# Hybrid decoder step on one core: the second dense group of a tick is placed straight behind the first

## What is computed

```python
def decoder_layer(x, c, attend, conv_prev, ...):
    sh1, sc1, gt1, sh2, sc2, gt2 = ada_mod(c, w_ada, b_ada)
    h = rms_norm(x, rms_g1) * (1 + sc1) + sh1
    q, k, v, hc, bgate, cgate, ga, gb = project_in(h, w_in, q_norm_g, k_norm_g)
    o_att = attend(q, k, v, sb_bias)
    yc, conv_state = short_conv(cgate * hc, conv_prev, conv_w, conv_b)
    x = x + gt1 * merge_branches(o_att, bgate * yc, ga, gb, w_att_out, w_conv_out, w_o)
    h2 = rms_norm(x, rms_g2) * (1 + sc2) + sh2
    x = x + gt2 * sqrelu_mlp(h2, w_mlp1, w_mlp2)
    return x, k, v, conv_state

def stick_breaking(z, valid):          # z = q.k/8 + bias
    log_beta = jax.nn.log_sigmoid(z)
    log_keep = jnp.where(valid, jax.nn.log_sigmoid(-z), 0.0)
    suffix = lax.cumsum(log_keep, axis=z.ndim - 1, reverse=True) - log_keep
    return jnp.where(valid, jnp.exp(log_beta + suffix), 0.0)
```

## Time and profile before

| | us |
|---|---|
| median of 3 runs | 1870.39 (1869.11 to 1870.75) |
| the profiled execution | 1871.02 |
| its span, first to last instruction | 1869.2 |
| TensorE busy | 1777.9 (95%) |
| VectorE busy | 878.6 (47%) |
| GpSimd busy | 659.8 (35%) |
| ScalarE busy | 299.3 (16%) |
| mean granted TensorE clock | 0.966 |

### The profile page before, as it was taken

One profiled execution on the slowest core, in us unless ns is written; L12 is line 12 of the kernel. 1 busy time (PEld: TensorE's weight loads), 2 busy tenths in 40 slices (PEclk: granted clock), 3 DMA queues, 4 the chain that ended last, 5 costly groups with the idle time before them and its releaser, 6 DMA issues. The chain is left out here.

```text
span 1869.2 us, 29718 instructions
## 1 busy us (share of the span) xinstructions
PE 1777.9 (95%) x11934; PEld 1657.0 (89%) x11934; DVE 878.6 (47%) x1425; ACT 299.3 (16%) x583; POOL 659.8 (35%) x377
## 2 busy tenths in 40 slices
PE   7999998997989999999898969999999999999999
PEld 6989777776778887879898868999999999999999
DVE  1434155545444444432783246555454545455553
ACT  3123211010101111111210123201020202020200
POOL 1037034343424443442342213433333333333332
PEclk8699999998989999999999989999999999999999
DMA  6312064444544665643432101111111111111112
GB/s 218 118 55 79 35 223 165 155 161 137 196 144 156 227 205 183 212 150 127 186 138 93 45 23 35 46 46 46 46 48 53 47 46 46 46 46 46 46 46 93
DMA packets 72505, 196.83 MB, mean 105 GB/s; under 512 B 8081, under 2 KB 8210, under 8 KB 72370
## 3 DMA queue, kind: packets, MB, share of 16 engines
q1 hardware_dynamic: 67682, 179.76, 28.6%
q10 hardware_dynamic: 4688, 15.18, 2.1%
HBM read 175.41 MB, written 19.50 MB: 104 GB/s over the span
## 5 line engine op out<-in xcount | busy, mean ns | idle before, releaser
L523 POOL TENSOR_TENSOR wh<-raw,zero 128x1024 fp32r<-128x1024 f32 x116 | 220.0, 1897 | 789.0 <-PE bank L589 700.3
L525 POOL TENSOR_TENSOR wl<-raw,wh 128x1024 fp32r<-128x1024 f32 x116 | 285.2, 2458 | 9.1
L589 PE MATMUL bank<-hH,wh 128*128 128x352 f32 x816 | 280.5, 344 | 3.0 <-POOL wl L525 3.0
L589 PE MATMUL bank<-hL,wh 128*128 128x352 f32 x816 | 266.5, 327 | 0.0
L589 PE MATMUL bank<-hH,wl 128*128 128x352 f32 x816 | 266.0, 326 | 0.0
L589 PE MATMUL bank<-h2H,wh 128*128 128x352 f32 x768 | 248.4, 323 | 0.9 <-issue 0.9
L1303 DVE SCALAR_TENSOR_TENSOR act<-bank,mods,act 128x352 f32<-128x352 f32 (+1 forms) x216 | 122.3, 571 | 268.0 <-PE bank L589 262.0
L589 PE MATMUL bank<-hidH,wh 128*128 128x352 f32 x768 | 247.7, 323 | 0.0
L589 PE MATMUL bank<-h2H,wl 128*128 128x352 f32 x768 | 246.3, 321 | 0.0
L550 POOL TENSOR_TENSOR beta<-beta,kb 128x512 f32<-128x512 f32 (+3 forms) x96 | 122.5, 1296 | 350.9 <-DVE kb L1132 350.9
L589 PE MATMUL bank<-hidH,wl 128*128 128x352 f32 x768 | 246.3, 321 | 0.0
(11 more groups left out here) (147 smaller groups left out, 2667.9 us busy)
## 6 DMA issues: line engine op xcount, KB each, us to landing
raw<-in_weights SPq DMA_DIRECT2D x168, 512.0 KB, 3.6
ring<-in_cache_k SPq DMA_DIRECT2D x128, 256.0 KB, 4.0
ring<-in_cache_v SPq DMA_DIRECT2D x128, 256.0 KB, 3.6
gate_scratch<-gt ACTq DMA_DIRECT2D x16, 528.0 KB, 3.7
act<-gate_scratch SPq DMA_DIRECT2D x16, 528.0 KB, 4.5
xt<-in_xT SPq DMA_DIRECT2D x8, 528.0 KB, 9.0
act<-in_xT SPq DMA_DIRECT2D x8, 528.0 KB, 4.5
out_yT<-act SPq DMA_DIRECT2D x8, 528.0 KB, 2.7
```

The costliest lines, as they stand in the source:

```text
L523: mark(pool.tensor_tensor(wh[u % 2][:, :], src[:, :], zero[:, 0:1].to_broadcast([P, 1024]), ALU.add))
L525: pool.tensor_tensor(wl[u % 2][:, :], src[:, :], wh[u % 2][:, :].bitcast(F32), ALU.subtract)\
L589: mm = pe.matmul(out, x, y, start=n == 0, stop=n == end)
```

## The change

In a tick with two dense groups, the second now comes directly behind the first on TensorE, ScalarE, VectorE and GpSimd, ahead of `sample_turn`, `sample_scores` and `turn`. `SLOTS`, from which the order of loads is made, is changed alike. No instruction is added or removed.

```diff
-SLOTS = ("scores", "dense_a", "sturn", "sscore", "turn", "dense_b", "ada", "av", "sav")
+SLOTS = ("scores", "dense_a", "dense_b", "sturn", "sscore", "turn", "ada", "av", "sav")
...
# gpsimd
                 if k in DENSE_A and DENSE_A[k] + 1 in ends:
                     split(ends[DENSE_A[k] + 1])
+                if k in DENSE_B and DENSE_B[k] + 1 in ends:
+                    split(ends[DENSE_B[k] + 1])
                 if k in ITEM_AT:
                     sample_a(ITEM_AT[k])
-                if k in DENSE_B and DENSE_B[k] + 1 in ends:
-                    split(ends[DENSE_B[k] + 1])
...
# tensor
                 if k in DENSE_A:
                     dense(DENSE_A[k], hH, hL)
+                if k in DENSE_B:
+                    dense(DENSE_B[k], hH, hL)
                 if k in TURN_AT:
                     sample_turn(TURN_AT[k], k)
                 if k in ITEM_AT:
                     sample_scores(ITEM_AT[k], k)
                 if 0 < k <= NSTEP:
                     turn(k - 1)
-                if k in DENSE_B:
-                    dense(DENSE_B[k], hH, hL)
...
# scalar
                 if k in DENSE_A:
                     evict(DENSE_A[k], k)
+                if k in DENSE_B:
+                    evict(DENSE_B[k], k)
                 if k in ITEM_AT:
                     sample_probability(ITEM_AT[k])
-                if k in DENSE_B:
-                    evict(DENSE_B[k], k)
...
# vector
                 if k in DENSE_A:
                     evict(DENSE_A[k])
+                if k in DENSE_B:
+                    evict(DENSE_B[k])
                 if k in TURN_AT:
                     sample_turned(TURN_AT[k])
                 if k in ITEM_AT:
                     sample_scan(ITEM_AT[k])
                 if 0 < k <= NSTEP:
                     turned(k - 1)
-                if k in DENSE_B:
-                    evict(DENSE_B[k])
```

## The result

The changed kernel takes 1920.69 us in the median of four runs (1910.59 to 1921.47) against 1869.89 for the kernel before: a ratio of 1.0266, 95% interval 1.0243 to 1.029. The sign and the kind of wait were forecast. The size was not: 1920.7 lies above the range of 1886 to 1916, +50.8 us where some 34 were forecast.

What follows compares the result with a forecast made beforehand. TensorE was taken to bound the middle stage. The profiled 1871.0 us plus 23.9 of waits, -1.6 for convolutions and 11.6 of clock gave 1904.9, or 1904.3 for the median; range 1886 to 1916.

Steps and rivals of the forecast that it cites:

- Terms 1 to 3: New waits of TensorE ahead of `values` in ticks with a second dense group, B: 23.9 us in all.
- term 1: Seven ticks where B's split runs beside VectorE's sample scan: `values` waits 1.6 us with `ada`, 3.4 without.
- term 2: Ticks 9, 12, 24, 27, 33, 36, 48, without `ada` or a split freed by B: new waits, 8.1 us.
- term 3: Ticks 1, 16, 25, 38, 40, with `ada` and a split freed by A: 0.2 us each, 1.0 in all.
- Term 4: Ticks 3, 8, 14, 19, where VectorE runs a convolution: -1.6 us in sum, between -5 and +4.
- Term 5: TensorE's clock falls behind the new waits, slowing matmuls: 11.6 us, possibly nothing or 20.
- The sign that would have made the term void: `sample_values` (L754) staying at 1.07 us behind the waits would mean no clock cost.
- The scan does not slip past the split: Denies the rival that VectorE's scan avoids the port conflict with GpSimd's split: 1879 us, chance 0.07.
- Long dense runs hold the clock: Rival: 48 matmuls in a row keep TensorE at 2.4 GHz through short waits: 1864 us, chance 0.04.
- the high case: Clock cost of 20 us, convolutions at +3 and 2 us of loads: 1919 us, cut to 1916.

Runs made afterwards that it cites:

- pool_back: Changed kernel with the GpSimd split freed by group B moved back behind sample_a, other engines as in the change: 1896.6 us.
- halfway: Changed kernel with group B moved only half as far, behind sample_scores but ahead of turn, and the split behind sample_a: 1873.3 us.
- filled kernels: Unneeded TensorE matmuls added in front of waits for VectorE: 322 in the changed kernel, 1886.3 us; 189 in the kernel before, 1853.4 us.
- after_conv_late: Changed kernel with VectorE's convolution moved last in its tick, behind the AT copies, modulation and out_block: 1885.9 us.

## Why the prediction was wrong in size, point by point

**Terms 1 to 3, the new waits: right.** The whole idle time rose by 26.75 us. Tick by tick in the changed trace, the new waits are 14.7 us for term 1 (14.8 forecast), 8.5 for term 2 (8.1) and 1.1 for term 3 (1.0), in all 24.3 where 23.9 were forecast. The waits of ticks 4 and 6 are 1.43 and 3.33, forecast 1.6 and 3.4. pool_back shows the cause of term 1, halfway what B had covered. Reading them from ticks of the old kernel that lacked B worked.

**Term 4, the convolutions: wrong sign.** It put -1.6 us; idle time alone came to +2.6 (7.35 - 4.52 in tick 8, 6.37 - 4.16 in 19, 5.46 - 4.82 in 3, 5.97 - 9.07 in 14). Tick 14 returned 3.1 us of idle time where 3.7 were put. In tick 8 I set the new wait off against slow-clock time that it would "replace". It replaced none: the clock fell there as before, only behind a longer wait. In tick 19 the wait was to grow by 0.3 and grew by 2.2. It begins 2.5 us behind the start of the convolution in place of 4.2, since `values` now waits itself and covers nothing, and it ends 8.9 behind it in place of 8.4, since the copies into `AT` follow the convolution.

**Term 5, the clock: the step that failed.** It put 11.6 us and "or 20" as its bound; the busy time of TensorE in the stage rose by 22.3 to 22.95. That this is the clock shows in the granted clock: TensorE's busy time in the stretches granted 1.2 GHz grew from 38.2 to 81.3 us, and half of that growth, 21.5 us, is what the full clock would have saved (an estimate). Told by place, each tick together with the one behind it, reckoned in the same way, the seven ticks of term 1 cost some 13 us, where 10.1 were put. Ticks 12, 24 and 36 cost 5.1, where 0.9 was put. Tick 16 cost 1.7, where nothing was put. Tick 14 cost 2.5 more than before, and the rest nearly cancels. Two things were missing from the term. `ada` was taken as 1.8 us at either level of the clock; behind a wait it takes 3.42 (ticks 8 and 14). And the slow stretch was ended at `sample_values`, but the `scores` and the dense group of the next tick are often in it; behind tick 24 nearly all of it lies there. The filled kernels confirm the term by taking it away: 29 to 34 us less for the changed kernel, 14 for the one before. The difference, 15 to 20, is somewhat below the 22.95, but the busy times without the fillers are equal. The sign that would have made the term void, L754 at 1.07 behind the waits, appeared only in some ticks, 6 among them; in ticks 8, 10, 14, 28, 30 and 32, for example, it takes 1.9.

**The rivals.** The scan does not slip past the split: it takes 2.58 us beside it in all seven ticks. (The 8.1 us of waits in that rival's sum leave out the 1.0 of term 3.) "Long dense runs hold the clock" is refuted as the order stands: 0.93, not above 0.96. The advice of the Trainium skill that I cited for it (TensorE: Matmul & The Clock Gate, HAM oscillation — how this bites in real kernels), to do matmuls together ahead of a wait, is given for loops that wait on loads. It is not contradicted. Keeping TensorE fed does hold the clock, as the filled kernels show with 0.99 and 1.00; keeping dense groups together did not keep it fed.

**The range.** Its upper end cut the high case from 1919 to 1916, "since not all comes together". Here it did: waits and slower clock came together, and their bounds should be added. A clock term of twice its size, with convolutions at +3, would have given about 1920.5.

Open: why the same wait costs clock in one execution and none in another, as in tick 6. Tick 10 has the same wait of 1.59 us in both kernels, and its twelve matmuls of `values` take 1.67 and 1.98 us. One of the four runs of the changed kernel took 1910.6 us at a clock of 0.959, the others 1920.7 to 1921.5 at 0.951 or 0.952; it wasn't profiled. So the clock term has a spread of its own of some 10 us, which the range did not allow for. How the slow clock behind a given wait divides between that wait and the small matmuls around it wasn't separated.

## What to carry to other kernels

Before two long pieces of work are put together, ask what the second one covered where it stood: here up to 4 us of VectorE's latency in each of 30 ticks, of which some 20 came to wait. Moving one engine's step moves its neighbours' too, and a step may then land on another engine's critical piece; nearly half of this loss (24 of 51 us) lay in the place of a GpSimd split that nobody waited for. Where TensorE waits, price the wait twice, once as idle time and once as slow clock behind it, small matmuls included. No fixed rate came out for the second: 22.3 us with 26.75 of idle time in the change, but only 6.5 with 14.3 and 7.5 with 22.0 given back in pool_back and after_conv_late, and none lost with 4.5 in halfway.

## What the runs showed of the hardware

- Matmuls whose results are thrown away made both kernels faster (29 to 34 us and 14 us), by filling waits behind which the clock fell: in the middle stage it rose from 0.93 to 0.99 and from 0.96 to 1.00.
- The small matmuls of `ada` (9 columns each, 16 records) take 1.85 us at the full clock and 3.42 behind a wait, 1.85 times as long, though they move hardly any columns.
- A wait of 0.28 us was followed by matmuls at the lower level of the clock (tick 16), and one of 3.33 us by matmuls at the full clock (tick 6 of the same execution).
- The convolution's tensor_scalar over 1024 elements (L1208) takes 0.81 us alone and 2.38 to 2.96 beside GpSimd's split in the kernel before. In tick 8 it takes 2.95 in the changed kernel and 0.81 with the split moved back on GpSimd alone, and the wait for the convolution is 3.2 us shorter.
